# A hybrid encoder layer on eight cores: spatial gate in the merges' banks, weight casts ahead of u, DMA transposes apart from their norm weight, early loads in quarters

## The chip, the cores and the metric

One Trainium2 chip, all 8 of its cores. Every core runs the same program on its own 10,240 tokens; no core waits for another. The metric is the device time of one execution on the slowest core, in microseconds.

## The reference, cut to what matters

Two request groups (32 x 2048 and 2 x 8192 tokens, 1024 channels) go through one layer with shared weights.

```python
h = rmsnorm(x, norm_pre_mix)
proj = h @ w_in                        # [f 512 | u 512 | v 512 | gate_a 1024 | gate_b 1024]
u, v = gelu(u), gelu(v)
gate_a, gate_b = sigmoid(gate_a), sigmoid(gate_b)
y_a = fourier_mix(f) @ w_fourier_out   # real 2-D DFT over positions and 128 channels per group
v = layernorm(v, ln_g, ln_b)           # then W_s (4 x 128 x 128) inside chunks of 128 positions
y_b = (u * (W_s v + b_s)) @ w_sgu_out
x = x + rmsnorm((gate_a * y_a + gate_b * y_b) @ w_o, norm_post_mix)
h2 = rmsnorm(x, norm_pre_ffn)
up = centred_depthwise_conv(h2 @ w_up, conv_w, conv_b)        # width 3
x = x + rmsnorm((gelu(up[:4096]) * up[4096:]) @ w_down, norm_post_ffn)
```

## The kernel before, in words

The program is written out by hand: `P.op(engine, ...)` appends an instruction to that engine's list, and each engine works its list strictly in order. Waits are derived from the names in `reads` and `writes` (a tile or a bank written waits for its last writer and all its readers). DMAs are issued from SP's queue ("sp") or from GpSimd's ("pool", the ones that cast f32 to bf16). So the order of calls in the source is the order of work on every queue.

PSUM has eight banks of 512 f32 columns. In the token mixer bank 0 is for transposes, banks 1 to 3 are a ring handed out by `wbank()`, and (4, 5), (6, 7) are the pairs `ypairs` of the out tiles and merges.

The work of a core runs in three stages.

*Fourier stage* (loop over n = 0 to 80, 128 tokens each, in the order of the DFT). Two tiles of x are loaded by one DMA (`xload`, 1 MB, four buffers), squared for the norm (`stats`), cast (`castx`, L714, on VectorE and GpSimd in turn), transposed on TensorE (L725), projected (`fproj`) and put through the first DFT step with table `t1` (`stage1`); results go to memory as Z (`zbig`, `zsmall`). Beside it SP loads what comes next: the rest of the table (`t1b`, n = 2), the Fourier weights `wfa` and `wfb` (n = 26), the small sequence's Z (`zload_small`, n = 19, four DMAs that wait for all four Z writes), and block 0's x (`pre_load`, n = 62). GpSimd issues the mixer's weights from n = 73 (`load_mixer_weights`: u, v, two quarters of the gates) and behind the loop (`load_mixer_weights_2`).

*Token mixer* (20 blocks of 512 tokens, p = 0 to 19). A block has, on TensorE:
- four u chunks (`proj_chunk`, 8 matmuls each, evacuated by an activation, L843);
- four times a v tile (8 matmuls, activation L852, norm on VectorE and GpSimd) and an out tile of the block before (`out_tile`, 16 matmuls into a pair);
- eight steps dc = 0 to 7 of a gate-a chunk, a gate-b chunk (8 matmuls and one activation each, into the ring) and, from dc = 2, a merge (`merge_chunk`, 8 matmuls into a pair, then L891 and L895 on VectorE and L898 on GpSimd); in dc = 0 and 1 the spatial gate's four groups (`sgu_group`, 4 x 128 columns into a bank of the ring, then L874 and L881 on VectorE) stand between them.

`close_tile` ends an out tile: it loads the residual into one of two buffers `xr` (SP), squares on ScalarE (L474), takes the root on GpSimd (L479, L481 on 128x1), scales on VectorE (L924), adds on GpSimd (L929), stores (SP). So the load for tile 2 waits for the store of tile 0, that for tile 3 for the store of tile 1.

Next to this runs the norm of the next block: `pre_load` (4 tiles into `xt`), `pre_square` (one behind each out tile), `pre_scale` (the row factors `rsd`, L479 and L481 on 128x4, on GpSimd behind the last L929), `pre_cast` (L527, ScalarE, xt times factor into one of two buffers `xs`), `pre_flip` (a DMA transpose from SP, L553, and right behind it on VectorE the product with the norm weight, L555). In blocks 0 to 3 the second DFT step (`big_steps`) is interleaved too; its copies L469 and L470 alternate between ScalarE and VectorE and its matmuls use the ring. From p = 4 GpSimd issues four casts of channel-mixer weights per block: `cast_wup` and `cast_wd` behind `pre_scale`, `cast_wd` in dc 2, `cast_wup` in dc 5.

*Handover and channel mixer.* The last block's four out tiles, the first up chunks and the halo of the convolution (rows of neighbouring blocks: `halo_load`, `halo_norm`, `turn`, `halo`) meet. Then for 20 blocks 32 up chunks of 16 matmuls (`up`, `conv`, L1111, L1123, L1131) and the down projection (L1194).

## Time and profile before

| | |
|---|---|
| three runs | 5138.63, 5149.03, 6016.25 us; median 5149.03 |
| profiled execution, its own time | 5129.78 us |
| its span on the slowest core (core 6) | 5128.2 us |
| spans of the eight cores | 5085.4 to 5128.2 us |
| granted clock of the cores, mean | 0.992 to 0.994 |
| TensorE busy | 4970.4 us, 97% |
| VectorE, ScalarE, GpSimd busy | 54%, 45%, 39% |
| DMA | 771.36 MB, mean 150 GB/s |

Times are from the start of the span of core 6. L463 is the line of the helper through which nearly all matmuls go, L448 that of nearly all DMAs, L474 that of all squares, L479 and L481 those of all roots. A group of matmuls in the timeline is a run without a wait; the bracket behind it is the idle time before it and who ended it. A few per cent of the matmul records are missing (a block has 336 matmuls, of which some 329 to 338 are seen). The granted clock is 1.00 at 2.4 GHz and 0.50 at 1.2 GHz.

### The profile page before, as it was taken

Reading aid. Unit: us, or ns where it says so; the run is one execution under the profiler, and the core shown is the slowest. Engines: PE = TensorE matmul, PEld = TensorE weight load, DVE = VectorE, ACT = ScalarE, POOL = GpSimd, SP = SyncE. Lnnn points to the kernel's source line nnn. Section 1 sums busy time; section 2 is a strip of 40 time slices with the busy share of each in tenths; the row PEclk is TensorE's granted clock in tenths of the full one; section 3 lists DMA queues with packets and bytes.
Section 4 is the critical chain, followed back from the end, with each engine's and each line's share of the span. In section 5 each row is a group of like instructions: output and inputs, shape, how many; then the busy total and the mean of one; then the engine's idle time right before and its main releaser. Section 6 shows DMA issues by size and latency. Waiting matters only on the chain.

```text
span 5128.2 us, 81411 instructions; the slowest of 8 cores (5085.4 to 5128.2 us)
## 1 busy us (share of the span) xinstructions
PE 4970.4 (97%) x23976; PEld 2307.1 (45%) x24457; DVE 2786.6 (54%) x3917; ACT 2310.8 (45%) x3516; POOL 1984.9 (39%) x2480
## 2 busy tenths in 40 slices
PE   7889999999999999999999999999999999999999
PEld 4434444444444444444444444444444444444444
DVE  4635444444454475556645674557655674557554
ACT  5634433433333354445544554445544554445433
POOL 2323344443444433333433343334433343334333
PEclk9999999999999999999999999999999999999999
DMA  9794566555655574434534454445444454435432
GB/s 289 251 181 130 160 128 126 138 135 124 136 128 141 127 238 143 141 124 161 165 136 137 130 189 134 142 127 165 154 138 128 147 177 136 144 124 177 145 124 98
DMA packets 476173, 771.36 MB, mean 150 GB/s; under 512 B 285751, under 2 KB 310455, under 8 KB 474590
## 3 DMA queue, kind: packets, MB, share of 16 engines
q1 hardware_dynamic: 384526, 689.65, 43.3%
q0 software_dynamic: 91216, 76.46, 8.1%
q8 instruction: 210, 3.44, 0.3%
q14 instruction: 221, 1.81, 0.1%
HBM read 655.27 MB, written 130.02 MB: 153 GB/s over the span
## 4 chain that ended last, share of the span: by engine, by line
PE 89%; DMA 5%; issue 3%; POOL 1%; DVE 1%; ACT 1%; SPq 0%; POOLq 0%; DVEq 0%; ACTq 0%
PE psum L463 67%; PE psum L1194 21%; DMA arena<-arena 1%; DMA arena<-xf 1%; DMA arena<-xn 1%; ACT arena L474 0%; POOL arena L929 0%; PE psum L725 0%; DMA arena<-zbig 0%; DVE arena L874 0%; POOL arena L481 0%; DMA x1s<-arena 0%; DMA zbig<-arena 0%; POOL arena L714 0%; SPq L448 0%
## 5 line engine op out<-in xcount | busy, mean ns | idle before, releaser
L463 PE MATMUL psum<-arena 128*128 128x512 bf16 (+3 forms) x18278 | 3838.0, 369 | 108.2 <-DVE arena L874 15.3
L463 PEld LDWEIGHTS psum<-arena 128*128 128x128 bf16 (+1 forms) x18657 | 1767.3, 99 | 2152.4 <-issue 136.2
L1123 DVE SCALAR_TENSOR_TENSOR arena<-psum,arena 128x511 f32<-128x511 f32 x2560 | 1751.0, 743 | 348.7 <-ACT arena L1111 348.5
L1111 ACT ACTIVATE arena<-psum,arena 128x512 f32<-128x512 f32 x1280 | 993.2, 776 | 746.6 <-PE psum L463 746.6
L1133 POOL TENSOR_TENSOR arena<-arena 128x512 bf16<-128x512 bf16 x640 | 745.7, 1165 | 939.7 <-ACT arena L1131 922.1
L1194 PE MATMUL psum<-arena 128*128 128x512 bf16 x5018 | 1102.8, 379 | 5.4
L924 DVE SCALAR_TENSOR_TENSOR arena<-psum,arena 128x1024 f32<-128x1024 f32 x159 | 204.1, 1284 | 1154.6 <-POOL arena L481 1145.9
L1194 PEld LDWEIGHTS psum<-arena 128*128 128x128 bf16 x5120 | 500.9, 98 | 603.9
L474 ACT ACTIVATE arena<-psum 128x1024 bf16<-128x1024 f32 x160 | 163.8, 1024 | 1157.6 <-PE psum L1194 958.7
L843 ACT ACTIVATE arena<-psum 128x512 bf16<-128x512 f32 x400 | 238.5, 596 | 640.9 <-PE psum L463 609.7
L929 POOL TENSOR_TENSOR arena<-arena 128x1024 f32<-128x1024 f32 x159 | 377.0, 2371 | 189.9 <-DVE arena L924 126.6
L1131 ACT ACTIVATE arena<-arena 128x512 bf16<-128x512 f32 x640 | 397.0, 620 | 65.3 <-POOL arena L1128 64.2
L479 POOL TENSOR_SCALAR arena<-arena 128x1 f32<-128x1 f32 (+2 forms) x241 | 52.2, 216 | 946.8 <-ACT arena L474 940.5
L898 POOL TENSOR_TENSOR arena<-arena 128x512 bf16<-128x512 f32 x160 | 226.0, 1413 | 452.2 <-DVE arena L895 452.1
L555 DVE TENSOR_TENSOR arena<-arena 128x1024 bf16<-128x1024 bf16 x156 | 199.1, 1276 | 238.6 <-DMA arena<-arena 238.6
L1128 POOL TENSOR_TENSOR arena<-arena 128x4 f32<-128x4 f32 x640 | 197.0, 308 | 270.8 <-DVE arena L1123 265.2
L474 ACT ACTIVATE arena<-arena 128x1024 bf16<-128x1024 f32 (+1 forms) x241 | 253.3, 1051 | 38.1 <-DMA arena<-xf 26.9
L527 ACT ACTIVATE arena<-arena 128x1024 bf16<-128x1024 f32 x160 | 182.3, 1139 | 32.3 <-DMA arena<-arena 31.7
L891 DVE SCALAR_TENSOR_TENSOR arena<-arena,psum 128x512 f32<-128x512 bf16 x160 | 109.5, 684 | 127.8 <-PE psum L463 123.6
L481 POOL TENSOR_TENSOR arena<-arena 128x1 f32<-128x1 f32 (+2 forms) x241 | 159.3, 661 | 35.7
L854 DVE BATCH_NORM_STATS2 arena<-arena 128x6 f32<-128x512 f32 x80 | 54.9, 686 | 158.3 <-ACT arena L852 158.3
L895 DVE SCALAR_TENSOR_TENSOR arena<-arena,psum 128x512 f32<-128x512 bf16 x160 | 109.5, 684 | 12.7 <-PE psum L463 3.7
(45 smaller groups left out, 975.7 us busy)
## 6 DMA issues: line engine op xcount, KB each, us to landing
arena<-wups SPq DMA_DIRECT2D x640, 512.0 KB, 3.5
arena<-xn SPq DMA_DIRECT2D x160, 512.0 KB, 6.6
arena<-x1s SPq DMA_DIRECT2D x160, 512.0 KB, 5.5
arena<-xf SPq DMA_DIRECT2D x40, 1024.0 KB, 11.7
x1s<-arena SPq DMA_DIRECT2D x80, 512.0 KB, 3.2
y<-arena POOLq DMA_DIRECT2D x79, 512.0 KB, 4.0
wups<-w_up POOLq DMA_DIRECT2D x64, 256.0 KB, 5.2
arena<-yscr SPq DMA_DIRECT2D x20, 512.0 KB, 4.0
```

The lines of the kernel that those rows point to most:

```text
L463: ins = e.matmul(out, lhsT=l, rhs=r, start=(i == 0), stop=(i == n - 1))
L474: P.op("act", lambda e: e.activation(out=sqjunk[:n, :], in_=src, func=AF.Square, accum_out=acc), reads=reads, writes=["sqjunk", accname])
L555: P.op("dve", lambda e: e.tensor_tensor(out=dst, in0=dst, in1=gvec.unsqueeze(2).broadcast_to([128, 8, 128]), op=ALU.mult), reads=[("hT", p ...
L843: P.op("act", lambda e: e.activation(out=dst, in_=bank(wb), func=func, scale=scale), reads=[("ps", wb)], writes=[dres])
L898: P.op("pool", lambda e: e.tensor_tensor(out=mT[:, dc, :], in0=tmp[k1], in1=tmp[k2], op=ALU.add), reads=[("tmp", k1), ("tmp", k2)], writes ...
L924: P.op("dve", lambda e: e.scalar_tensor_tensor(out=tt[k], in0=po, scalar=rsd2[s2][:, 0:1], in1=gpo, op0=ALU.mult, op1=ALU.mult), reads=pr ...
L929: P.op("pool", lambda e: e.tensor_tensor(out=xr[k2], in0=tt[k], in1=xr[k2], op=ALU.add), reads=[("tt", k), ("xr", k2)], writes=[("xr", k2)])
L1111: P.op("act", lambda e, half=half, b=b, c=c: e.activation(out=cv2[:, half, :], in_=bank(b), func=AF.Identity, bias=cst[:, C_CB + c:C_CB + ...
L1123: P.op("dve", lambda e, o_=o_, i_=i_, wt=wt: e.scalar_tensor_tensor(out=o_, in0=i_, scalar=wt, in1=o_, op0=ALU.mult, op1=ALU.add), reads=[ ...
L1131: P.op("act", lambda e: e.activation(out=gg, in_=cv2[:, 0, :], func=AF.Gelu_apprx_tanh), reads=[("cgv", k, 0)], writes=[("gg", k)])
L1133: P.op("pool", lambda e: e.tensor_tensor(out=actT[:, j, :], in0=gg, in1=cv2[:, 1, :], op=ALU.mult), reads=[("gg", k), ("cgv", k, 1)], writ ...
L1194: P.op("pe", lambda e, dh=dh: [e.matmul(bank(b0 + dh), lhsT=actT[:, j, t * 128:(t + 1) * 128], rhs=wd[j // 4][:, j % 4, dh * 512:(dh + 1) ...
```

## The change

Seven edits.
1. `sgu_group(h)` writes bank 4 + h, one of the merges' banks, instead of the next of the ring.
2. The four weight casts of a block (p >= 4) are issued together at its start, ahead of u.
3. `pre_flip` issues only the DMA transpose; the product with the norm weight is `pre_gain`, called later. For p = 4 to 18 there are four buffers `xs`, casts and transposes stand in dc 0 to 3 and the products in dc 4 to 7. For p = 1 to 3 and 19, casts and transposes stand in dc 1 to 4 and the products two steps behind. In the channel mixer the casts move from every second chunk from 18 on to every second from 17 on.
4. In block 0 the v tiles come ahead of the u chunks, `winv` is loaded ahead of `winu`, and its transposes go over TensorE (`pre_turn`).
5. In the Fourier stage `t1b`, `wfa`, `wfb`, the small Z and block 0's x are loaded in quarters at chosen n, each with a name of its own.
6. At the handover up chunk 0 stands ahead of out tile 0, and the halo's norm and transpose ahead of the last tails; the residuals of tiles 0 and 1 are loaded in the last block's dc 7 (`xr_load`).
7. `prep_wfo` moves to n = 35, 43, 53, 63.

```diff
-    xs = [at(16 + 2 * k, D, BF16, [("xs", k)]) for k in range(2)]
+    xs = [at((16, 18, 60, 62)[k], D, BF16, [("xs", k)]) for k in range(4)]
...
-    def pre_flip(par, t, gvec):
+    def pre_gain(par, t, gvec):
         dst = hTb[par][:, :, t * 128:(t + 1) * 128]
-        src = xs[t % 2]
-
-        def flip(eng, sem):
-            eng.dma_start_transpose(out=dst, in_=src).then_inc(sem, 16)
-        P.op("sp", flip, reads=[("xs", t % 2)], writes=[("hT", par, t)], ndma=1)
         P.op("dve", lambda e: e.tensor_tensor(
             out=dst, in0=dst, in1=gvec.unsqueeze(2).broadcast_to([128, 8, 128]), op=ALU.mult),
             reads=[("hT", par, t), "cst0"], writes=[("hT", par, t)])
+
+    def pre_flip(par, t, nx=2):
+        dst = hTb[par][:, :, t * 128:(t + 1) * 128]
+        src = xs[t % nx]
+
+        def flip(eng, sem):
+            eng.dma_start_transpose(out=dst, in_=src).then_inc(sem, 16)
+        P.op("sp", flip, reads=[("xs", t % nx)], writes=[("hT", par, t)], ndma=1)
...
-        ld_w(winu, ["winu"], w_cols(0, 512), [("axb", 2)])
-        ld_w(winv, ["winv"], w_cols(512, 512))
+        ld_w(winv, ["winv"], w_cols(512, 512), [("axb", 2)])
+        ld_w(winu, ["winu"], w_cols(0, 512))
...
-        if n == 2:
-            P.op("sp", dma1(t1[:, 0:64, :], t1v[:, 0:64, :]), writes=["t1b"], ndma=1)
+        if n in (2, 12, 28, 44):
...
-        if n == 26:
...
+        if n in (24, 32, 40, 50):
...
+        if n in (19, 25, 33, 41):
+            zload_small((19, 25, 33, 41).index(n))
...
-        if n == 62:
-            pre_load(0, xn, blocks[0])
+        if n in (37, 47, 57, 65):
+            pre_load(0, xn, blocks[0], None, [(37, 47, 57, 65).index(n)])
...
     def sgu_group(h):
-        wb = wbank()
+        wb = 4 + h
...
+        if p >= 4:
+            cast_wd(1)
+            cast_wup(1)
+            cast_wd(1)
+            cast_wup(1)
...
+        if p > 0:
+            u_chunks()
         add = None
         for t in range(4):
             v_tile(par, t)
...
         if add is not None:
             add()
-        if p > 0:
+        if p == 0:
+            u_chunks()
+        else:
             pre_scale(1 - par)
-        if p >= 4:
-            cast_wup(1)
-            cast_wd(1)
...
-            late = 3 if p == 0 else 0
-            if 3 + late <= dc < 7 + late:
-                pre_flip(1 - par, dc - 3 - late, nxt[3])
-            if 2 + late <= dc < 6 + late:
-                pre_cast(1 - par, dc - 2 - late)
+            if p == 0:
+                if 6 <= dc:
+                    pre_turn(1 - par, dc - 6, nxt[3])
+                if 5 <= dc:
+                    pre_cast(1 - par, dc - 5)
+            elif 4 <= p < NBLK - 1:
+                if dc < 4:
+                    pre_cast(1 - par, dc, 4)
+                    pre_flip(1 - par, dc, 4)
+                else:
+                    pre_gain(1 - par, dc - 4, nxt[3])
+            else:
+                if 1 <= dc < 5:
+                    if dc >= 3:
+                        pre_gain(1 - par, dc - 3, nxt[3])
+                    pre_cast(1 - par, dc - 1)
+                    pre_flip(1 - par, dc - 1)
+                elif 5 <= dc < 7:
+                    pre_gain(1 - par, dc - 3, nxt[3])
...
-            if p >= 4 and dc == 2:
-                cast_wd(1)
-            if p >= 4 and dc == 5:
-                cast_wup(1)
...
     last = blocks[-1]
-    out_tile(last, 0, (6, 7))()()
+    fins = [conv(0, 0, up(0, 0))]
+    out_tile(last, 0, (6, 7), xr_last[0])()()
     halo_load(1)
-    fins = [conv(0, 0, up(0, 0))]
     fins.append(conv(0, 1, up(0, 1)))
-    tail = out_tile(last, 1, (6, 7))
     halo_norm()
+    out_tile(last, 1, (6, 7), xr_last[1])()()
+    out_tile(last, 2, (1, 2))()()
+    tail = out_tile(last, 3, (3, 4))
+    turn(0, NH, hhT[:, :, :], "hhT", gpf, 0)
     tail()()
-    out_tile(last, 2, (1, 2))()()
-    out_tile(last, 3, (3, 4))()()
-    turn(0, NH, hhT[:, :, :], "hhT", gpf, 0)
```

ScalarE in a steady block (p from 4 on), from the last out tile's square on. L474 on psum is that square, L474 on arena the square of the next block's tile, L843 the activations of gate and u chunks, L527 the cast. Before:

```order
L474 ACTIVATE arena<-psum 128x1024 [waits sem_pe,sem_act]
L474 ACTIVATE arena<-arena 128x1024 [waits dsem27,sem_act]
L843 ACTIVATE arena<-psum 128x512 [waits sem_pe] x6
L527 ACTIVATE arena<-arena 128x1024 [waits dsem21,sem_pool]
L843 ACTIVATE arena<-psum 128x512 [waits sem_pe] x2
L527 ACTIVATE arena<-arena 128x1024 [waits dsem22]
L843 ACTIVATE arena<-psum 128x512 [waits sem_pe,sem_act,sem_dve] x2
```

Of the change at the same place (L849 is the activation, L528 the cast):

```order
L474 ACTIVATE arena<-psum 128x1024 [waits sem_pe,sem_act]
L474 ACTIVATE arena<-arena 128x1024 [waits dsem15,sem_act]
L849 ACTIVATE arena<-psum 128x512 [waits sem_pe] x2
L528 ACTIVATE arena<-arena 128x1024 [waits dsem7,sem_pool]
L849 ACTIVATE arena<-psum 128x512 [waits sem_pe] x2
L528 ACTIVATE arena<-arena 128x1024 [waits dsem8]
L849 ACTIVATE arena<-psum 128x512 [waits sem_pe] x2
```

The first cast, which waits for GpSimd's row factors, stood behind six activations and stands now behind two.

GpSimd in a steady block, from the last residual adds (L929) to the next block's first norm of v (L857). Before:

```order
L929 TENSOR_TENSOR arena<-arena 128x1024 x2
L479 TENSOR_SCALAR arena<-arena 128x4
L481 TENSOR_TENSOR arena<-arena 128x4
L495 DMA wups<-w_up 1024x1x128 x2
L448 DMA wds<-w_down 16x8192
L898 TENSOR_TENSOR arena<-arena 128x512
L448 DMA wds<-w_down 16x8192
L898 TENSOR_TENSOR arena<-arena 128x512 x3
L495 DMA wups<-w_up 1024x1x128 x2
L898 TENSOR_TENSOR arena<-arena 128x512 x4
L857 TENSOR_SCALAR arena<-arena 128x1
```

Of the change (L940 is the residual add, L904 the merge's sum, L863 the norm of v):

```order
L940 TENSOR_TENSOR arena<-arena 128x1024 x2
L479 TENSOR_SCALAR arena<-arena 128x4
L481 TENSOR_TENSOR arena<-arena 128x4
L904 TENSOR_TENSOR arena<-arena 128x512 x8
L448 DMA wds<-w_down 16x8192
L495 DMA wups<-w_up 1024x1x128 x2
L448 DMA wds<-w_down 16x8192
L495 DMA wups<-w_up 1024x1x128 x2
L863 TENSOR_SCALAR arena<-arena 128x1
```

The casts left the merges and stand together behind the block's last merge; the row factors stand where they stood, behind the last residual add.

SP in the Fourier stage, from the load of the small Z on. Before:

```order
L448 DMA arena<-zsmall 128x4x512 x4
L448 DMA arena<-xf 128x2x1024
L448 DMA zbig<-arena 128x2048
L448 DMA arena<-xf 128x2x1024
L448 DMA arena<-sgb 128x512
L448 DMA arena<-xf 128x2x1024
L448 DMA zbig<-arena 128x2048
L448 DMA arena<-xf 128x2x1024
L448 DMA arena<-w_foA 128x4x1024
L448 DMA arena<-w_foB 128x4x1024
```

Of the change:

```order
L448 DMA arena<-zsmall 128x4x512
L448 DMA arena<-xf 128x2x1024
L448 DMA zbig<-arena 128x2048
L448 DMA arena<-xf 128x2x1024
L448 DMA arena<-sgb 128x512
L448 DMA arena<-xf 128x2x1024
L448 DMA arena<-w_foA 128x1024
L448 DMA arena<-w_foB 128x1024
L448 DMA zbig<-arena 128x2048
L448 DMA arena<-zsmall 128x4x512
L448 DMA arena<-xf 128x2x1024 x2
L448 DMA arena<-t 128x2048
```

One load of a quarter stands at each place, and the others follow between later xf loads.

## Rows read from the trace of the kernel before

**Rows 1.** The page: busy time of each engine.
```profile
PE 4970.4 (97%) x23976; PEld 2307.1 (45%) x24457; DVE 2786.6 (54%) x3917; ACT 2310.8 (45%) x3516; POOL 1984.9 (39%) x2480
```
**Rows 2.** TensorE by stretch: us, busy, instructions, granted clock, DMA share, GB/s.
```profile
20.00:264.70 244.70, 207.12 (x1444) 0.96 0.89 271
150.00:200.00 50.00, 48.69 (x356) 1.00 0.75 252
264.70:348.60 83.90, 65.24 (x307) 0.91 1.02 169
348.60:631.60 283.00, 262.16 (x1390) 0.97 0.51 151
631.60:1715.30 1083.70, 1052.85 (x4942) 1.00 0.59 132
1756.00:1812.00 56.00, 42.38 (x248) 0.88 0.36 122
1812.00:5128.20 3316.20, 3290.69 (x15394) 1.00 0.45 147
```
**Rows 3.** TensorE's waits, 0 to 1900 us: in total, times, longest.
```profile
PE psum L725 <- DVE arena L714: 22.7, 6, 7.9
...
PE psum L725 <- POOL arena L714: 12.4, 19, 2.9
...
PE psum L463 <- DVE arena L541: 6.8, 1, 6.8
```
**Rows 4.** Timeline of all engines, one steady block: start, us, instruction, idle before.
```profile
1357.48 0.33 SPq L448 DMA_DIRECT2D x1s<-arena  x1
...
1358.08 1.02 ACT L474 ACTIVATE arena<-psum 128x1024 bf16<-128x1024 f32 x1 [2.34 <-PE psum L463]
...
1362.44 9.24 PE L463 MATMUL psum<-arena 128*128 128x512 bf16 x47 [0.61 <-DVE arena L874]
...
1364.94 2.36 POOL L929 TENSOR_TENSOR arena<-arena 128x1024 f32<-128x1024 f32 x1 [2.36 <-DMA arena<-xn]
...
1368.04 1.03 POOL L481 TENSOR_TENSOR arena<-arena 128x4 f32<-128x4 f32 x1
1368.32 0.60 ACT L843 ACTIVATE arena<-psum 128x512 bf16<-128x512 f32 x1 [1.35 <-PE psum L463]
...
1370.54 1.14 ACT L527 ACTIVATE arena<-arena 128x1024 bf16<-128x1024 f32 x1
```
**Rows 5.** TensorE's timeline at four places.
```profile
302.36 3.83 PE L463 MATMUL psum<-arena 128*128 128x512 bf16 x17 [0.91 <-DVE arena L891]
...
349.19 34.14 PE L463 MATMUL psum<-arena 128*128 128x512 bf16 x169 [6.16 <-DVE arena L555]
...
1168.00 49.99 PE L463 MATMUL psum<-arena 128*128 128x512 bf16 x219 [3.65 <-DVE arena L891]
...
1648.96 70.12 PE L463 MATMUL psum<-arena 128*128 128x512 bf16 x329 [0.61 <-DVE arena L874]
```
**Rows 6.** GpSimd's timeline: row factors of the first and the last steady block.
```profile
643.60 1.02 POOL L481 TENSOR_TENSOR arena<-arena 128x4 f32<-128x4 f32 x1
...
1725.02 1.02 POOL L481 TENSOR_TENSOR arena<-arena 128x4 f32<-128x4 f32 x1
```
**Rows 7.** DMA issues of 1371.5 to 1373 and of 1386 to 1390 us.
```profile
arena<-arena SPq DMA_TRANSPOSE x1, 13.4
...
arena<-arena SPq DMA_TRANSPOSE x2, 3.4
```
**Rows 8.** TensorE by stretch, behind the wait that ends at 1168.00.
```profile
1168.00:1172.00 4.00, 4.00 (x10) 0.50 0.48 93
1172.00:1176.00 4.00, 3.95 (x15) 0.80 0.24 46
```
**Rows 9.** SP's timeline, the small Z.
```profile
76.58 2.02 SPq L448 DMA_DIRECT2D arena<-zsmall  x4
```
**Rows 10.** DMA issues of 260.1 to 260.85 us.
```profile
arena<-w_so POOLq DMA_DIRECT2D x1, 1024.0 KB, 42.0
```

More of the change, by code:

```diff
@@ L508, in build_program, with pre_load @@
     pre_slot = {}
[L510 to L511 removed]
+    def pre_load(par, src, i, srcname=None, tiles=range(4)):
+        for t in tiles:
             P.op("sp", dma1(xt[t], src[i * BLK + t * 128:i * BLK + (t + 1) * 128, :]),
                  reads=[(srcname, i, t)] if srcname else [], writes=[("xt", t)], ndma=1)
[L514 removed]
+        if tiles[-1] == 3:
+            pre_slot[par] = ring("css", 3)
     def pre_square(par, t):
@@ L694, in prep_wfo @@
             out=wfo[:, c, :], in0=wfb[:, c, :], scalar=cst[:, C_WS + c:C_WS + c + 1], in1=wfa[:, c, :],
-            op0=ALU.mult, op1=ALU.add), reads=["wfa", "wfb", "cst"], writes=[("wfo", c)])
+            op0=ALU.mult, op1=ALU.add), reads=[("wfa", c), ("wfb", c), "cst"], writes=[("wfo", c)])
     def prep_bmat():
```

69 lines of the change are left out of this document (37 added, 32 removed).

## The prediction

> **What bounds the kernel now.** I read the page first, then the granted clock and busy time stretch by stretch, then TensorE's waits, then one block of the token mixer in order of time on all engines. The page says that TensorE is the bound: busy 4970.4 of 5128.2 us [rows 1]. An average hides where the rest is, so the stretches come next [rows 2]. From 1812 us to the end, the channel mixer, TensorE is busy 3290.7 of 3316.2 us at full granted clock: nothing the change does there can be worth more than a few us, and I count that stretch as unchanged. All that can be won lies before 1812 us. The reader should see four stretches with idle time: the Fourier stage to 264.7 us, the first block of the token mixer to 348.6, the three blocks that still carry the second DFT stage to 631.6, and the handover from 1756 to 1812. The steady blocks between look full (1052.85 of 1083.7 us), but they count most, because there are 15 of them and whatever one gains or loses is paid 15 times.
>
> The waits of TensorE [rows 3] name the causes: late casts of x in the Fourier stage (L714 on VectorE and GpSimd), and one long wait for the halo's transpose (L541). Inside the blocks they are short and come from VectorE: the spatial gate's evacuation (L874), merge arithmetic (L891), second-stage copies (L470).
>
> **Steady blocks, the part that decides.** Let T be the start on ScalarE of the last out tile's square, which is also when TensorE leaves that tile; the block in [rows 4] has T = 1358.08. What the change takes away here: the spatial gate leaves the ring of three banks, so the 0.61 us wait on L874 at the second gate chunk goes [rows 4], with a second one on L874 that some blocks have; and the norm weight no longer stands on VectorE right behind each DMA transpose, so the waits on L891 go (one of them is 3.65 us [rows 5]). A block without any wait beyond the 0.61 us runs 329 recorded matmuls in 70.12 us plus that wait [rows 5]. The 15 periods from T = 631.6 to T = 1715.3 take 1083.7 us [rows 2], 72.25 each, so the excess is (72.25 - 70.12) x 15 = 32 us, and I let all of it go.
>
> What it adds: the first cast of the next block's tile (L527) now stands on ScalarE behind two gate activations instead of six. It needs the row factors, and these come from GpSimd's L481 on 128x4, which stands behind the residual add L929 of the last out tile, which waits for a load into a buffer whose store must land first. In [rows 4] the store goes out at 1357.48, the load behind it ends the add's wait at 1364.94 and L481 ends at 1369.07, T + 11.0. Over the sixteen blocks from p = 4 it ends between T + 9.8 and T + 13.8, mean 11.6; [rows 6] has the first of them, T = 631.6, with T + 13.0, and the last, T = 1715.3, with T + 10.7. Nothing in the change shortens this chain. In the kernel before, the cast starts at T + 12.5 in most blocks, just behind it, and holds nobody.
>
> Now who is queued behind the cast? The activation of the second gate-a chunk, and its bank is the one that the third gate-b chunk needs (a ring of three). TensorE comes to that chunk at about T + 9.6: in [rows 4] the activation of the chunk before it starts at 1368.32, T + 10.2, and 0.61 us of that is the wait that goes. The bank comes free when the factors are there, plus a cast (1.14 us) plus an activation (0.60 us). With the factors at T + 11.6 that is T + 13.3, a wait of 3.7 us. I add 0.6 us because the weight casts, which now go out as one burst at the start of the block, will still be in the DMA engines when the first store of the chain leaves: in [rows 7] a transpose issued among them took 13.4 us to land and those issued without them 3.4 us. So 4.3 us x 15 blocks (p = 4 to 18; the last block keeps two buffers and casts one chunk later) = 65 us.
>
> After such a wait the granted clock drops. TensorE resumes at 1168.00 after that wait of 3.65 us and then has 0.50 (1.2 GHz) for 4 us and 0.80 for 4 us: 2.0 + 0.8 = 2.8 us lost [rows 8]. The 0.61 us waits cost no clock: the steady blocks as a whole have 1.00 [rows 2]. I take 2.3 us x 15 = 35 us, with bounds 0 and 2.8 us a block. Steady blocks: 65 + 35 - 32 = +68 us. Bounds: factors at T + 9.8 and no loss of clock give 1.9 x 15 - 32 = -4 us; T + 13.8 with 2.8 us of clock gives (5.9 + 2.8) x 15 - 32 = +98 us. The moved weight casts themselves cost nothing where they stand: their issuing lies on GpSimd while TensorE does the four u chunks and one v tile, 40 of the block's matmuls or 8.5 us by [rows 5], and nothing but the first v tile's norm stands behind them.
>
> **Fourier stage.** Of 244.7 us TensorE is busy 207.1, at 0.96 of the clock [rows 2]. Most of the idle time is three gaps behind late xf loads, with 22.7 us on L714 on VectorE and part of the 12.4 us on GpSimd [rows 3]. Bursts on SP go ahead of them: the small-sequence load of Z waits for its last write, so its four issues start only at 76.58 and end at 78.60 [rows 9], and behind it come wfa and wfb (4 MB at once) and block 0's x (2 MB). The change breaks these up but moves no fewer bytes. The DMA engines are busy 0.89 of the stage at 271 GB/s [rows 2], so kept full they would still need 0.89 x 244.7 = 218 us: at most 27 us can be won. Where TensorE runs unhindered, 150 to 200 us, they are busy 0.75 at 252 GB/s [rows 2], so some 80 GB/s are spare. The quarters put about 10 MB (4 of wf, 2 of Z, 1.6 of the table, 2 of x) into 110 us from the first Z load on, 91 GB/s, a little more than that. I take -20 us; bounds 0 and -27. The first Z load still blocks SP, since it still waits for all four writes.
>
> **First block.** v ahead of u hides the chain of the v norms. But the weights behind it come from GpSimd's queue: w_so was issued at 260.2 and landed 42.0 us later, at 302.2 [rows 10], and TensorE resumes with the first merge's second half at 302.36 [rows 5]. That is a wait on a DMA whatever stands ahead, so I count nothing for v ahead of u. The four transposes on TensorE instead of the DMA remove the 6.16 us wait on L555 at 349.19 [rows 5] and a shorter one on L470 behind the first of them, and add 4 x 0.45 us of transposes and about 2.5 us in which the next block waits for the last one's VectorE step. With the clock regained: -7 us; bounds +3 and -18.
>
> **Blocks p = 1 to 3.** 283 us with 262.16 busy at 0.97 [rows 2]. Here the cast comes one chunk later (dc 1) and the second-stage copies that share the ring with it fall to VectorE, so ScalarE is held 3 us but TensorE hardly. -8 us; bounds +8 and -20.
>
> **Handover.** Two up chunks now stand ahead of and between the out tiles, and the halo's transpose no longer waits on VectorE for the last tile. The first out tile's wait for its last merge and the 6.8 us on L541 go [rows 3], and of the 56 us, busy 42.38 at 0.88 of the clock [rows 2], some 5 us of clock come back. Some idle time behind the halo stays, since tiles 2 and 3 still load behind stores. -12 us; bounds -2 and -16.
>
> **Sum.** 68 - 20 - 7 - 8 - 12 = +21 us on 5129.8, the profiled execution's own time: 5151. The three times shown are 5138.6, 5149.0 and 6016.3; 5149.0 is the median and the profiled run lies below all three, so I give 5155. About 2% is what a measurement of this kernel can tell from no change.
>
> **Rivals.**
> (a) *The casts hold nobody.* The factors would have to end by T + 7.9, so that cast and activation are done by T + 9.6. For it: much of the chain is DMA time, a store that leaves at 1357.48 and a load that ends the add's wait at 1364.94 [rows 4], and it could shrink where the engines are quiet. Against: none of the sixteen blocks is earlier than T + 9.8. Then the steady blocks give -32: 5129.8 - 79 = 5051, measured some 5055.
> (b) *The burst of weight casts pushes the chain* (slower side). Place: start of each block from p = 4, where 3 MB of loads start too; a transpose among three such casts landed 10 us late [rows 7], so four of them with the loads may last until T, 28 us on. Each us by which the factors come later than the T + 12.2 of the sum costs 15 us. At T + 16: 3.8 x 15 = +57, 5208; it passes no-change against the sum above at once, and 2% from T + 19 on.
> The Trainium skill (DMA: Bandwidth & Descriptors, Queues, rings and completion order) says that each DMA engine serves the queues that have work in turn, a packet at a time. By that rule a software-queue burst takes turns with every load and store of SP, which is this rival; the slow transpose above agrees with it.
> (c) *The early stages gain nothing*, because bytes and not bursts bind them: Fourier and first block 0, all else as forecast: 5129.8 + 48 = 5178.
>
> **How the numbers follow.** Forecast 0.55, (a) 0.17, (b) 0.17, (c) 0.11. The likeliest case has 5110 to 5190 from its own bounds. The range reaches down to 5075, short of most of (a), and up to 5220, over (b) and (c). Faster by over 2% (under 5046) needs (a) and more: 0.05. Slower by over 2% (over 5252) needs (b) at its worst: 0.05. The rest 0.90.
>
> **What would show it.** In the changed profile: in each of the 15 steady blocks one wait of TensorE of 3 to 6 us before the third gate-b chunk, released by a gate activation on ScalarE; ScalarE idle up to the cast and released by GpSimd's 128x4 power; half clock behind it; no waits on the spatial gate's evacuation and almost none on L891; a period near 76 to 77 us. In the Fourier stage the three gaps shrink to a few us and it ends near 245 us. The halo's wait is gone. The forecast is wrong if the period of the steady blocks is under 72 us, if the factors come by T + 8, or if the gate-b chunk waits for something other than that activation.

## The result, and the profile of the changed kernel

The changed kernel is 1.6% slower: ratio to the kernel before 1.016, 95% interval 1.0115 to 1.0205. Its profiled execution took 5226.95 us (span 5225.4) against 5129.8 (5128.2), so 97 us more where I forecast 21. The direction was right and the size was not: 5225 lies just above the range. (The chip ran some executions of every kernel with one or both dies slowed; their times are left out, and of a profile taken in such an execution only the blocks or cores that it spared are read.)

First the page of the changed kernel. The reader should see TensorE's idle time before its matmuls (the last number of a group) and what ended most of it, and at the bottom the time that weight casts and stores take to land.

```profile
PE 5025.0 (96%) x24489; PEld 2314.4 (44%) x24489; DVE 2798.7 (54%) x3917; ACT 2306.2 (44%) x3516; POOL 2022.1 (39%) x2480
...
L463 PE MATMUL psum<-arena 128*128 128x512 bf16 (+3 forms) x18657 | 3888.4, 371 | 165.2 <-ACT arena L849 108.1
...
L528 ACT ACTIVATE arena<-arena 128x1024 bf16<-128x1024 f32 x160 | 182.3, 1140 | 168.5 <-POOL arena L481 163.4
...
x1s<-arena SPq DMA_DIRECT2D x80, 512.0 KB, 4.0
...
wups<-w_up POOLq DMA_DIRECT2D x64, 256.0 KB, 19.0
```

In the kernel before, the same matmul group stood idle for 108.2 us, and the weight casts landed after 5.2 us:

```profile
L463 PE MATMUL psum<-arena 128*128 128x512 bf16 (+3 forms) x18278 | 3838.0, 369 | 108.2 <-DVE arena L874 15.3
...
wups<-w_up POOLq DMA_DIRECT2D x64, 256.0 KB, 5.2
```

So two things stand out: 108.1 us behind gate activations (L849, before L843), with ScalarE itself idle 163.4 us behind the row factors (L481), and weight casts that take 19 us. The waits of TensorE up to 2000 us, to be held against [rows 3], say how often:

```profile
PE psum L463 <- ACT arena L849: 108.1, 16, 11.5
PE psum L728 <- DVE arena L717: 13.0, 7, 3.5
PE psum L728 <- POOL arena L717: 11.8, 16, 3.0
...
PE psum L463 <- DVE arena L1116: 7.4, 2, 6.9
PE psum L463 <- ACT arena L858: 7.3, 1, 7.3
PE psum L463 <- DVE arena L542: 5.3, 2, 3.2
PE psum L463 <- DMA arena<-wups: 4.2, 1, 4.2
PE psum L463 <- DMA arena<-w_so: 2.3, 1, 2.3
```

Sixteen waits, one in each block from p = 4 on (the last, in p = 19, is of 3.1 us). Here is one, in the timeline of all engines; T = 1413.69 (start of the last out tile's square).

```profile
1408.21 0.33 SPq L448 DMA_DIRECT2D x1s<-arena  x1
...
1413.16 0.33 SPq L448 DMA_DIRECT2D arena<-xn  x1
...
1413.60 0.37 SPq L448 DMA_DIRECT2D x1s<-arena  x1
1413.69 1.02 ACT L474 ACTIVATE arena<-psum 128x1024 bf16<-128x1024 f32 x1 [2.34 <-PE psum L463]
...
1417.76 2.35 POOL L940 TENSOR_TENSOR arena<-arena 128x1024 f32<-128x1024 f32 x1 [1.91 <-DMA arena<-xn]
...
1418.95 0.33 SPq L448 DMA_DIRECT2D arena<-xn  x1
...
1422.97 2.80 POOL L940 TENSOR_TENSOR arena<-arena 128x1024 f32<-128x1024 f32 x1 [2.87 <-DVE arena L880]
...
1426.52 1.02 POOL L481 TENSOR_TENSOR arena<-arena 128x4 f32<-128x4 f32 x1
1427.64 1.15 ACT L528 ACTIVATE arena<-arena 128x1024 bf16<-128x1024 f32 x1 [9.73 <-POOL arena L481]
1428.69 1.06 ACT L849 ACTIVATE arena<-psum 128x512 bf16<-128x512 f32 x2
...
1429.41 10.87 PE L463 MATMUL psum<-arena 128*128 128x512 bf16 x39 [6.35 <-ACT arena L849]
```

Read it from below: TensorE waits 6.35 us for a gate activation, which stands behind the cast, which had ScalarE idle for 9.73 us until the factors ended at 1427.54, T + 13.85. (L849 x2 merges two activations in one row.) Then follow the chain up. The store issued at 1413.60 lets the next load go at 1418.95, 5.35 us later; in [rows 4] the store left at 1357.48 and its load at 1360.93, 3.45 later (the row below, from the trace of before). The 2.87 us before the last add are put down to VectorE's L880, which had long been done; what came last was that load. The mechanism is the one forecast, with a slower DMA in it.

```profile
1360.93 0.33 SPq L448 DMA_DIRECT2D arena<-xn  x1
```

Over the 15 steady blocks of this core the factors end at T + 14.5 in the mean (T + 12.7 to T + 19.0), against T + 11.6 before, and the waits have a mean of 7.0 us: longest in the first block, 11.46, shortest 5.18. Each wait is the factors' end, counted from T, minus 7.5 us (18.96 and 11.46 in the first block, 13.85 and 6.35 here; 7.2 to 7.6 in all). My sum had minus 7.9, so its rule held and was 0.4 us short.

Granted clock behind the wait at 1429.41: 0.50 (1.2 GHz) for 4 us, then 0.92 for 4, where [rows 8] had 0.50 and 0.80. The run behind it lasts 72.41 us for 336 matmuls. A block without any wait takes 69.96 (the base among the experiments): 2.45 us lost.

```profile
1429.41:1433.41 4.00, 4.00 (x10) 0.50 0.69 135
1433.41:1437.41 4.00, 4.00 (x19) 0.92 0.34 66
1437.41:1441.41 4.00, 4.00 (x20) 1.00 0.00 0
```

Where the time went, stage by stage, as the mean of all eight cores (the slowest alone in brackets). The marks are TensorE's end of the Fourier stage, ScalarE's first activation of the second block, T of the first steady block, and T of the last block.

| | Fourier ends | second block | first steady T | 15 periods | last T to end |
|---|---|---|---|---|---|
| before | 261.5 | 347.2 | 621.4 (631.6) | 1071.0 (1083.8) | 3414.5 (3412.9) |
| changed | 252.4 | 333.1 | 603.4 (614.0) | 1183.1 (1192.7) | 3417.2 (3418.6) |

For the slowest core: -17.6 up to the first steady block, +108.9 in the 15 periods, +5.7 behind, 97 together. Another kernel with the same early code as before gave 626.6 for the first steady T, and seven with the early code of the change 599.1 to 608.8, so differences of 5 us at that mark are noise. Split at the marks and in the mean of the cores, the 18 us won before the first steady block are 9.1 in the Fourier stage, 5.0 in the first block and 3.9 in the next three.

### The profile page after: what moved, and what is told of

Read it like the earlier page. It is cut to its first block, busy times and chain, and to the rows that moved or that the text cites. A ratio compares the mean times of both kernels' runs of the same rounds, so it can differ in the third digit from the quotient of the medians.

```text
span 5225.4 us, 82027 instructions; the slowest of 8 cores (5189.4 to 5225.4 us)
## 1 busy us (share of the span) xinstructions
PE 5025.0 (96%) x24489; PEld 2314.4 (44%) x24489; DVE 2798.7 (54%) x3917; ACT 2306.2 (44%) x3516; POOL 2022.1 (39%) x2480
## 4 chain that ended last, share of the span: by engine, by line
PE 85%; DMA 9%; POOL 3%; issue 2%; ACT 1%; SPq 0%; DVE 0%; POOLq 0%; ACTq 0%; DVEq 0%
PE psum L463 63%; PE psum L1225 21%; DMA x1s<-arena 3%; DMA arena<-xn 2%; POOL arena L940 2%; DMA arena<-xf 1%; DMA arena<-w_so 1%; DMA arena<-zbig 1%; POOL arena L481 1%; ACT arena L474 1%; PE psum L728 0%; SPq L448 0%; POOL arena L479 0%; DMA yscr<-arena 0%; DMA arena<-w_fT 0%
## 5 line engine op out<-in xcount | busy, mean ns | idle before, releaser
L463 PE MATMUL psum<-arena 128*128 128x512 bf16 (+3 forms) x18657 | 3888.4, 371 | 165.2 <-ACT arena L849 108.1
L935 DVE SCALAR_TENSOR_TENSOR arena<-psum,arena 128x1024 f32<-128x1024 f32 x159 | 204.1, 1284 | 1147.5 <-POOL arena L481 1141.5
L474 ACT ACTIVATE arena<-psum 128x1024 bf16<-128x1024 f32 x160 | 164.0, 1025 | 1144.1 <-PE psum L1225 958.6
L849 ACT ACTIVATE arena<-psum 128x512 bf16<-128x512 f32 x400 | 236.3, 595 | 607.1 <-PE psum L463 602.7
L904 POOL TENSOR_TENSOR arena<-arena 128x512 bf16<-128x512 f32 x160 | 262.7, 1642 | 539.5 <-DVE arena L901 539.5
L940 POOL TENSOR_TENSOR arena<-arena 128x1024 f32<-128x1024 f32 x159 | 376.9, 2370 | 241.5 <-DVE arena L935 127.0
L897 DVE SCALAR_TENSOR_TENSOR arena<-arena,psum 128x512 f32<-128x512 bf16 x160 | 109.9, 687 | 426.7 <-PE psum L463 356.9
L474 ACT ACTIVATE arena<-arena 128x1024 bf16<-128x1024 f32 (+1 forms) x241 | 253.5, 1052 | 33.5 <-DMA arena<-xf 17.0
L528 ACT ACTIVATE arena<-arena 128x1024 bf16<-128x1024 f32 x160 | 182.3, 1140 | 168.5 <-POOL arena L481 163.4
L481 POOL TENSOR_TENSOR arena<-arena 128x1 f32<-128x1 f32 (+2 forms) x241 | 158.8, 659 | 36.6 <-POOL arena L479 1.8
L901 DVE SCALAR_TENSOR_TENSOR arena<-arena,psum 128x512 f32<-128x512 bf16 x160 | 109.9, 687 | 25.6 <-PE psum L463 9.3
```

Of the source, the lines that this page charges most:

```text
L463: ins = e.matmul(out, lhsT=l, rhs=r, start=(i == 0), stop=(i == n - 1))
L474: P.op("act", lambda e: e.activation(out=sqjunk[:n, :], in_=src, func=AF.Square, accum_out=acc), reads=reads, writes=["sqjunk", accname])
L481: P.op("pool", lambda e: e.tensor_tensor(out=out, in0=out, in1=neghalf[:p, 0:n], op=ALU.pow), reads=[name, "neghalf"], writes=[name])
L849: P.op("act", lambda e: e.activation(out=dst, in_=bank(wb), func=func, scale=scale), reads=[("ps", wb)], writes=[dres])
L904: P.op("pool", lambda e: e.tensor_tensor(out=mT[:, dc, :], in0=tmp[k1], in1=tmp[k2], op=ALU.add), reads=[("tmp", k1), ("tmp", k2)], writes ...
L935: P.op("dve", lambda e: e.scalar_tensor_tensor(out=tt[k], in0=po, scalar=rsd2[s2][:, 0:1], in1=gpo, op0=ALU.mult, op1=ALU.mult), reads=pr ...
```

## The experiments

The theory from this profile: the cast stands too early on ScalarE and waits for factors that come at the end of the chain of store, load and add; and the burst of weight casts delays that chain. The rivals: the burst costs by itself, whoever waits; or the factors are late for another reason. Four kernels, all made from the changed one, took these apart.

**Casts of x moved back.**

```diff
             elif 4 <= p < NBLK - 1:
-                if dc < 4:
-                    pre_cast(1 - par, dc, 4)
-                    pre_flip(1 - par, dc, 4)
-                else:
+                if dc >= 4:
                     pre_gain(1 - par, dc - 4, nxt[3])
+                if 2 <= dc < 6:
+                    pre_cast(1 - par, dc - 2, 4)
+                    pre_flip(1 - par, dc - 2, 4)
```

> The changed kernel with one thing moved back: in the steady blocks the four casts and flips stand behind the third to sixth gate-b chunk (as in the kernel before) instead of the first to fourth; gains stay apart, four cast buffers stay, the weight casts stay in a burst. T is the start on ScalarE of the last out tile's square. Theory (the wait is ScalarE held by a cast that stands too early for its factors): the waits before the third gate-b chunk (7.0 us a block, longest 11.5) go, with the half clock behind them; some 1 us stays where the factors end later than T+13, so the period falls from 79.2 to about 71.5 us and the time from 5226 to about 5110 (5100 to 5130). Rival (the burst of weight casts costs by itself, whoever waits): the factors still come at T+14 to 15 and the wait moves two chunks on, 3 us or more a block; 5160 or above.

Times 5091 to 5098; ratio to the kernel before 0.988 (0.977 to 0.999). The 15 periods take 70.37 us each in the mean of the cores, against 78.87 of the changed kernel. The factors come later than ever, T + 15.5 in the mean of the cores, and hold nearly nobody. The timeline below is of one block, T = 1393.11. The first store of the chain goes out at 1388.12 and the load behind it only at 1395.70; that load ends the wait of the last add but one, and everything behind it is late:

```profile
1395.70 0.33 SPq L448 DMA_DIRECT2D arena<-xn  x1
...
1400.35 2.89 POOL L940 TENSOR_TENSOR arena<-arena 128x1024 f32<-128x1024 f32 x1 [5.08 <-DMA arena<-xn]
...
1408.06 1.02 POOL L481 TENSOR_TENSOR arena<-arena 128x4 f32<-128x4 f32 x1
...
1409.18 1.15 ACT L528 ACTIVATE arena<-arena 128x1024 bf16<-128x1024 f32 x1 [4.27 <-POOL arena L481]
```

ScalarE idles 4.27 us here and TensorE does not notice: with the cast two chunks later, six gate activations are out of its way. The whole loss of the steady blocks goes with the place of the cast. It also shows that the waits were not what made the factors late, since without them they are later still.

**Weight casts moved back.**

```diff
-        if p >= 4:
-            cast_wd(1)
-            cast_wup(1)
-            cast_wd(1)
-            cast_wup(1)
...
             pre_scale(1 - par)
+        if p >= 4:
+            cast_wup(1)
+            cast_wd(1)
...
+            if p >= 4 and dc == 2:
+                cast_wd(1)
+            if p >= 4 and dc == 5:
+                cast_wup(1)
```

> The changed kernel with the four weight casts of each block back at the places of the kernel before (one pair behind the row factors, one behind the third chunk, one behind the sixth); the early casts of x stay. Theory (the burst in the DMA engines delays the store and the load ahead of the factors): the factors come back from T+14.4 (mean of 15 blocks) to T+11.6 to 12.2, the wait before the third gate-b chunk from 7.0 to about 4 us, store landing from some 5.3 to 3.4 us; period about 76.5, time 5226 - 15 x 2.8 = 5184 (5175 to 5200). Rival (the factors are late for another reason, such as the loads that start at the block's start or the waits themselves): they stay at T+14, time 5215 to 5226.

Times 5157 to 5181, ratio 1.007 (1.001 to 1.013): some 50 us under the changed kernel. In the four steady blocks read here the factors end at T + 10.5, 11.2, 10.6 and 10.7, and TensorE's waits are these and one of 3.23:

```profile
612.71 71.54 PE L463 MATMUL psum<-arena 128*128 128x512 bf16 x336 [2.97 <-ACT arena L849]
687.97 71.46 PE L463 MATMUL psum<-arena 128*128 128x512 bf16 x336 [3.71 <-ACT arena L849]
762.48 7.83 PE L463 MATMUL psum<-arena 128*128 128x512 bf16 x28 [3.05 <-ACT arena L849]
```

The period is 74.8 us, 70.0 + 3.2 + 1.6 of clock, against 78.9 in the mean of the changed kernel: 4.1 us a block for the burst, 62 in fifteen. That only some 50 show in the time would fit a last block that is 12 to 15 us longer with the weight casts at their old places, as in the run with both edits below; this profile can't show it. Without the burst TensorE waits 3.2 us, where my sum had 3.7 before its addition for the burst.

**Row factors ahead of the last residual add on GpSimd.**

```diff
+        if p > 0:
+            pre_scale(1 - par)
         if add is not None:
             add()
         if p == 0:
             u_chunks()
-        else:
-            pre_scale(1 - par)
```

> The changed kernel with one line moved: on GpSimd the row factors of the next block (128x4) stand ahead of the last out tile's residual add instead of behind it, so they need only the four squares of x. Theory (the chain store, load, add, factors is what holds the cast): factors at about T+4, casts hold nobody, waits before the third gate-b chunk 0 to 0.6 us, period 70.5 to 71, time 5226 - 15 x 8.4 = 5100 (5085 to 5115), under the kernel before. Rival (the four loads of x or their squares are themselves late, or the bank is held by something else): waits of over 3 us stay, time over 5170.

Times 5086 to 5114 and one of 5145; ratio 0.991 (0.986 to 0.996). On the slowest core the factors end at T + 6.3 in 12 of the 15 blocks and the wait is gone; over all eight cores they have a mean of T + 7.4, 24 waits of over 1 us are left in the 120 blocks, and the period is 70.7 us. The last residual add now stands behind the factors:

```profile
848.34 1.02 POOL L481 TENSOR_TENSOR arena<-arena 128x4 f32<-128x4 f32 x1
849.34 2.48 POOL L940 TENSOR_TENSOR arena<-arena 128x1024 f32<-128x1024 f32 x1
849.46 1.15 ACT L528 ACTIVATE arena<-arena 128x1024 bf16<-128x1024 f32 x1 [2.14 <-POOL arena L481]
```

Behind the last wait of that core, which ends at 779.82, TensorE runs without another for 620 us, up to the end of this view:

```profile
779.82 620.43 PE L463 MATMUL psum<-arena 128*128 128x512 bf16 x2957 [4.70 <-ACT arena L849]
```

I had expected T + 4. The factors still stand behind the add of the last tile but one, which waits for a load too, and in the first three steady blocks of this core, that load is late: factors at T + 11.1, 10.5, 12.2 and waits of 3.59, 2.95, 4.70, again the end minus 7.5. (Why the burst weighs most in the first of these blocks, here and in the changed kernel, is left open.)

**Both: factors first and weight casts back.**

> Both of the last two edits: factors ahead of the last residual add, and the weight casts back at the places of the kernel before. Theory (the burst costs only through the factors): the same time as with the factors moved alone, within 8 us. Rival (the burst also delays loads that others wait for, or early blocks): 10 to 30 us less than with the factors moved alone.

Times 5095 to 5098, ratio 0.988 (0.977 to 0.9995), the same as with the factors alone. The 15 periods have a mean of 69.96 us on seven cores and 70.02 on one, with the factors at T + 6.3. It gains 11 us there over the last run and loses 14.5 behind the last T, where TensorE waits 12.4 us on an activation in the last block. That made it a good base: what is left shows alone.

**The burst alone, in the kernel before.** The four casts moved to the block's start and nothing else: the diff under "Weight casts moved back" the other way round, applied to the kernel before.

> The kernel before with one thing of the change: the four weight casts of each block from the fifth on stand in a burst behind the block's loads. Theory (burst makes the factors late, and lateness costs only where the cast stands early): the row factors move from T+11.6 to T+14 to 16, as with the burst in the changed kernel; the casts of x at dc 2 come up to 3 us later, ScalarE is held a little, TensorE little or not: period 72 to 73, time 5115 to 5150. Rival (the burst costs TensorE wherever the casts stand, by late loads and stores): 3 us a block, 5160 or above.

5121 and 5127 us, beside 5129 and 5174 of the kernel before. The factors move from T + 11.3 to T + 14.0 in the mean of the cores, and the period is 71.1 us against 71.4. So the burst delays the chain here too, by 2.7 us (in the changed kernel by 3.4: T + 14.1 in the mean of the cores against T + 10.7 in the four blocks with the weight casts back), and costs nothing as long as no cast of x stands early: the rival falls.

What the burst does in the DMA engines is seen in their share just ahead of T. Below, TensorE by stretch with the DMA share and GB/s last, from T - 12 to T - 4, in the kernel before, in the run with the casts of x moved back and in the changed kernel. Before, they are nearly idle. With the burst the share is over 1, so packets overlap in time, and the first store of the chain, at T - 5.7 in the mean, starts into this.

```profile
1346.08:1354.08 8.00, 8.00 (x38) 1.00 0.13 51
```
```profile
1381.11:1389.11 8.00, 8.00 (x38) 1.00 1.18 176
```
```profile
1401.69:1409.69 8.00, 8.00 (x38) 1.00 1.47 217
```

The rule cited in rival (b), from the Trainium skill (DMA: Bandwidth & Descriptors, Queues, rings and completion order), says that an engine serves the queues with work in turn; these rows agree with it, though they don't show the order of packets.

How the delay travels is seen in the issues and landings of the steady blocks on all cores (112 of 120, whose stores the trace has). In the changed kernel the last weight cast lands at T - 2.0 in the mean. The first store (T - 5.7) runs among them and takes 4.8 us instead of 3.0. Its load therefore leaves at T - 0.8 instead of T - 2.6, just ahead of the second store (T + 0.0). In 98 of the 112 blocks no weight cast is left when that one is issued, and it still takes 5.5 us instead of 3.5. So the burst reaches the last add mostly through the first store. That the late load is what slows the second store fits the times, but no run shows it.

**Early loads back, on that base** (t1, small Z, wfa and wfb, block 0's x as before; one of the five edits shown).

```diff
-        if n in (37, 47, 57, 65):
-            pre_load(0, xn, blocks[0], None, [(37, 47, 57, 65).index(n)])
+        if n == 62:
+            pre_load(0, xn, blocks[0])
```

> Factors first and weight casts back (the fourth run, 5098, whose 15 steady periods were all 69.96 us, so that what is left shows up alone), with the early loads of the Fourier stage as in the kernel before: t1 in one piece, the small Z in four loads at once, wfa and wfb whole, block 0's x in one go. My sum had 20 us for them, bounds 0 and 27; the traces of the changed kernels show 5 to 14. Theory: the Fourier stage ends 5 to 10 us later and the first steady block starts at 620 to 630 instead of 615. Rival (the stage is bound by bytes, not bursts): within 3 us.

5100 and 5108. On four cores the Fourier stage ends at 262.1 instead of 253.6, and the first steady T is 609.6 instead of 605.1 (606.7 on the same four cores of the base). The loads in quarters are worth 8.5 us where they are. At the first steady block 3 to 4.5 us are left of it, which is within the noise at that mark.

**First block back, on that base** (u first, transposes by DMA).

```diff
-        if p > 0:
-            u_chunks()
+        u_chunks()
...
-        if p == 0:
-            u_chunks()
...
-                    pre_turn(1 - par, dc - 6, nxt[3])
+                    pre_flip(1 - par, dc - 6)
+                    pre_gain(1 - par, dc - 6, nxt[3])
...
```

The load of `winu` goes ahead of that of `winv` again, and the transposes of tiles 2 and 3 are changed in the same way.

> The same base (factors first, weight casts back) with the first block as in the kernel before: u ahead of v, winu loaded first, the four transposes for the second block by DMA. Theory (v first is worth nothing, the transposes on TensorE some 7 us): the first block takes 80 to 86 us instead of 80, the second starts with a wait of 4 to 6 us on the last gain; 3 to 8 us in all. Rival: no difference, since w_so lands late anyway.

5112 and 5118. From the end of the Fourier stage to the second block's first activation 87.9 us instead of 80.3: the new first block is worth 7.6 us.

**Only u ahead of v again** (the edit above, with all four transposes left on TensorE).

> Factors first and weight casts back (the fourth run), with u ahead of v again in the first block (and winu loaded first); the four transposes stay on TensorE. In the traces of the changed kernels the first block begins with a wait of 7 to 8 us, because the first v tile's activation writes where the last store of Z still reads; v first was meant to hide the norms, and I had counted it as nothing because w_so lands late. Theory (nothing: the 7 us go, and TensorE then waits longer for w_so): the first block takes as long as in the base, 79 to 82 us from TensorE's start to the second block's first u chunk, time 5095 to 5100. Rival (the new wait is on the path): 5 to 7 us less.

5092 and 5093, ratio 0.991 (0.988 to 0.995); the same stretch takes 79.6 us on four cores. So v first is worth nothing, and all 7.6 us are the transposes on TensorE. In the changed kernel the first v activation had ScalarE idle until the last store of Z was done, and TensorE waits for it, and then still for w_so:

```profile
271.49 1.09 ACT L858 ACTIVATE arena<-psum 128x512 f32<-128x512 f32 x2 [12.32 <-DMA zbig<-arena]
...
272.23 23.23 PE L463 MATMUL psum<-arena 128*128 128x512 bf16 x108 [7.26 <-ACT arena L858]
...
297.78 2.53 PE L463 MATMUL psum<-arena 128*128 128x512 bf16 x11 [2.32 <-DMA arena<-w_so]
```

**Last block's casts and handover as before, on that base.**

The diff shows the handover. The last block's casts of x go back to dc 2 to 5, each with its transpose one step later and the product right behind that.

```diff
...
-    fins = [conv(0, 0, up(0, 0))]
-    out_tile(last, 0, (6, 7), xr_last[0])()()
+    out_tile(last, 0, (6, 7))()()
     halo_load(1)
+    fins = [conv(0, 0, up(0, 0))]
     fins.append(conv(0, 1, up(0, 1)))
+    tail = out_tile(last, 1, (6, 7))
     halo_norm()
-    out_tile(last, 1, (6, 7), xr_last[1])()()
+    tail()()
     out_tile(last, 2, (1, 2))()()
-    tail = out_tile(last, 3, (3, 4))
+    out_tile(last, 3, (3, 4))()()
     turn(0, NH, hhT[:, :, :], "hhT", gpf, 0)
-    tail()()
```

> The same base with the last block's casts (from the third chunk, flip one chunk later, gain right behind) and the whole handover as in the kernel before. In the base TensorE waited 12.4 us in the last block, because the third cast needed a buffer whose transpose, issued behind the four loads of up weights, took long to land, and then 7.8 + 3.2 + 4.0 us in the handover. Theory: the 12 us go, with their half clock, and the handover costs what it did before (one wait of 6.8 us and others): 5098 - 15 = 5083, the kernel that beats both. Rival (the reordered handover was worth the 12 us I gave it): 5090 to 5098.

5087 us, a single time. The wait in the last block did not go, it only changed its name; neither theory nor rival. From the timeline:

```profile
1666.74 1.76 POOL L495 DMA_DIRECT2D wups<-w_up  x2
1667.36 5.07 SPq L448 DMA_DIRECT2D arena<-wups  x4
...
1672.59 26.18 SPq L560 DMA_TRANSPOSE arena<-arena  x4
...
1693.28 1.23 DVE L551 TENSOR_TENSOR arena<-arena 128x1024 bf16<-128x1024 bf16 x1 [21.57 <-DMA arena<-arena]
...
1695.24 17.28 PE L463 MATMUL psum<-arena 128*128 128x512 bf16 x72 [10.53 <-DVE arena L897]
```

The first transpose goes out at 1672.59 among weight casts and the four 512 KB loads of up weights of the last block, and takes 20.6 us to land; the merge on VectorE (L897) stands behind its product, which starts at 1693.28. The kernel before has the same transfers together at nearly the same place, the first transpose at T + 13.7 instead of T + 14.5 on the slowest cores. There it took 9.3 us (8.8 to 13.8 on the eight cores, against 19.3 to 22.6 here). What differs is that here the factors are early and so the weight casts leave at T + 8.7, ahead of the four loads (T + 9.3), and there at T + 10.4 to 12.8, behind the first of them. Whether this order is the reason is open.

**A clean last block**, with its four weight casts in a burst at its start (nothing waits there) and casts of x from the third chunk: once with the new handover, once with the one of before, and once with that and u first.

```diff
+        if p == NBLK - 1:
+            cast_wd(1)
+            cast_wup(1)
+            cast_wd(1)
+            cast_wup(1)
...
-        if p >= 4:
+        if 4 <= p < NBLK - 1:
             cast_wup(1)
             cast_wd(1)
...
```

> The same base with a clean last block: its four weight casts in a burst at its start instead of among the up weights' loads and the transposes, and its casts of x from the third chunk on, as in the kernel before; handover as changed (two up chunks among the out tiles, early loads for two of them, halo transpose before the last tile's tail). Theory: the waits of 10 to 12 us in the last block go with their half clock; from the last block's T to the end 3415 us instead of 3430, time 5084. Rival (transposes in the last block are slow because of the four loads of up weights): waits stay, 5095.

> As the run above, with the handover of the kernel before. My sum had 12 us for the new handover; the changed kernel's traces show 3 us on the other side. Theory (the new one is worth nothing or costs some, since the tiles behind the halo still load behind stores): 3408 to 3413 us from the last block's T to the end, time 5080, equal to the new one or 2 to 6 us less. Rival (the old one costs 12 us more, as I predicted): 5096.

> The run above with u ahead of v in the first block. Expected to be the fastest if the wait of 7 us on the first v tile is on the path: 5075; otherwise as the run above within 4 us.

New handover: 5079 and 5100 us, 3415.3 from the last T to the end. Old handover: 5071 and 5071, 3413.2, ratio to the kernel before 0.987 (0.984 to 0.991): the fastest, faster than both. With u first: 5076 and 5078, nothing gained. The long waits of the last block are gone (longest left in it on the slowest core of the first run: 1.0 us), and its first transpose, now beside the four loads without weight casts, lands after 7.4 to 8.7 us. In the new handover behind it waits of 3.2, 7.0 and 4.0 us stay. So the new handover is worth nothing, or costs 2 us. TensorE's timeline shows its waits, in the changed kernel, and below them those of the old handover in the fastest run:

```profile
1880.95 0.61 PE L463 MATMUL psum<-arena 128*128 128x40 bf16 x16 [3.24 <-DVE arena L542]
...
1888.47 0.69 PE L463 MATMUL psum<-arena 128*128 128x40 bf16 x16 [6.90 <-DVE arena L1116]
...
1900.71 2.62 PE L463 MATMUL psum<-arena 128*128 128x512 bf16 x8 [4.20 <-DMA arena<-wups]
```
```profile
1731.05 0.69 PE L463 MATMUL psum<-arena 128*128 128x40 bf16 x16 [6.72 <-DVE arena L542]
1732.23 0.69 PE L463 MATMUL psum<-arena 128*128 128x40 bf16 x16 [0.50 <-DVE arena L1128]
```

The 6.8 us behind the halo's transpose became 3.24, and a new wait of 6.90 stands one step on: the evacuation of the first halo product (L1116) is queued on VectorE behind the last out tile's L935 (at 1886.89), which waits for a root on GpSimd behind the residual add of the tile before, and that waits 4.51 us for its load.

## Why the prediction was wrong

*Steady blocks, +68; measured +109.* The mechanism is as put down: one wait a block before the third gate-b chunk, released by a gate activation, ScalarE idle up to the cast, half clock behind, no waits on the spatial gate's evacuation and none on the merges left. Three of its terms hold: 3.7 us of wait with factors at T + 11.6 (3.0 to 3.7 with T + 10.5 to 11.2 when the burst is taken away; by the measured rule it would be 4.1), 2.3 us of clock (2.45 measured), and 32 us of excess that goes (34 on the slowest core: 72.25 to 69.96 us a block in the base, times 15). The term that failed is "I add 0.6 us because the weight casts ... will still be in the DMA engines when the first store of the chain leaves": they push the factors by 2.9 us, to T + 14.5, beyond T + 13.8, which I had taken as the upper bound from one core (core 1 of the same trace has a block at T + 14.5). A wait of 7.0 x 15 = 105 us instead of 65 makes up the 41 us missing here: 2.3 us a block from the later factors, 0.4 from TensorE coming to the chunk at that much less than I had read. I had the price of this, 15 us for each us, in rival (b), and gave it 17 in 100. What I should have read is that the engines are nearly idle ahead of the chain in the kernel before (the 0.13 share above): the chain of before was measured in quiet engines, so its latest case was no bound for one in a burst. I had the 13.4 us transpose [rows 7] as a sign of it and took a small part of it.

*Fourier stage, -20; measured -8.5 to -9.1 at its end.* The three gaps did shrink (from 5.2, 7.9 and 6.3 us to 2.0, 3.0 and 3.5). The step that failed is the size of the term: I took 20 us, most of a bound of 27. The bound itself was no bound, since it took a DMA share of 1.00 as full, and a row with the burst has 1.47 at 217 GB/s. The same stretch of the changed kernel, to be held against the first line of [rows 2]:

```profile
20.00:259.40 239.40, 214.54 (x1472) 0.94 0.95 278
```

The DMA share rose from 0.89 to 0.95 and the rate from 271 to 278 GB/s. (The 0.94 of clock is that of this core; from 20 to 245 us the eight cores have a mean clock of 0.95 before and 0.97 in the changed kernel, so the clock did not take the gain.) That bytes bind the stage, as rival (c) said, fits a rate that hardly rises, but no run shows it; (c) was half true.

*First block, -7; measured -7.6* in the run with the old first block, -5.0 between the marks of the two kernels, and v ahead of u nothing, as counted. The reason given for that (w_so lands late) holds, with a second one that I had not seen: the first v activation waits for the last store of Z, whose source its buffer overlaps.

*Blocks p = 1 to 3, -8; measured about -3,* the table's second block to first steady T, 274.2 before and 271.4 in the mean of seven kernels with the change's early code.

*Handover, -12; measured +2, from the two clean runs.* The step that failed: "the halo's transpose no longer waits". It waits less, and the next instruction waits instead. I had said that some idle time stays since tiles 2 and 3 load behind stores, and did not follow who on VectorE stands behind them.

In sum, on the slowest core, 41 us were missed in the steady blocks and 35 in the rest (17 up to the first steady block, 18 behind the last T).

## What to carry to other kernels

An operation moved ahead on an in-order engine needs its input to be ready there in the worst state of its chain, not the mean one; moving the *producer* ahead instead (here the row factors, past an add that waited for a DMA) took away nearly all of the loss for one line (a period of 70.7 us), as did moving the casts back (70.4). And a chain that contains DMAs must be costed with the transfers that the same change puts beside it: its duration in the old trace is one in an old neighbourhood. An edit that holds in the steady turns of a loop can fail in its last turn (here by 10 to 12 us), so the first and the last turn are looked at apart.

## What the runs showed of the hardware that I had not expected

A burst of four weight casts (six DMAs, 1.57 MB in the software queue's row), issued from T - 25.6 to T - 22.2, holds up a plain 512 KB store issued 16 us behind it (4.8 us instead of 3.0), and the next store too, most often after the last cast has landed (5.5 instead of 3.5). From the first store to its load it was 7.6 us in the block with the casts of x moved back. The casts of w_up themselves take 19.0 us instead of 5.2 (medians). A DMA transpose issued among weight casts and four 512 KB loads took 20.6 us, 7.4 to 8.7 beside those loads without weight casts, and 3.4 without either [rows 7]. And with the waits taken away the cores run 15 blocks at 69.96 us each (70.02 on one): the 72.25 of the slowest core before holds 2.3 us of small waits, and even the best of the other cores had 70.9.
